# A new order for the chunks of the linear-attention heads in a two-layer hybrid decoder step

## The reference

```
S_t = e^{g_t} S_{t-1} + beta_t k_t (v_t - e^{g_t} S_{t-1}^T k_t)^T,   o_t = S_t^T q_t

# by chunks: q, k, v are the chunk's rows, gc the running sum of g in the chunk
decay = exp(gc_i - gc_j) for i >= j, else 0
L     = strictly lower part of (beta * k) k^T * decay
A     = L + I
u     = A^{-1} (v * beta)
w     = A^{-1} (k * beta * exp(gc))
qk    = (q k^T) * decay
# carried from chunk to chunk
v_new = u - w S
o     = (q * exp(gc)) S + qk v_new
S     = S * exp(gc_last) + (k * exp(gc_last - gc))^T v_new
```

## Time and profile before

| | us |
|---|---|
| median of 3 runs | 3143.12 |
| lowest and highest | 3142.41, 3145.15 |
| profiled execution, its own time | 3144.2 |
| span of the profiled execution | 3142.5 |
| TensorE busy in the span | 2954.7 (94%) |
| VectorE busy | 1398.7 (45%) |
| ScalarE busy | 610.6 (19%) |

### The profile page before, as it was taken

One profiled execution on the slowest core, in us unless ns is written; L12 is line 12 of the kernel. 1 busy time (PEld: TensorE's weight loads), 2 busy tenths in 40 slices (PEclk: granted clock), 3 DMA queues, 4 the chain that ended last, 5 costly groups with the idle time before them and its releaser, 6 DMA issues.

```text
span 3142.5 us, 46028 instructions
## 1 busy us (share of the span) xinstructions
PE 2954.7 (94%) x16570; PEld 2409.3 (77%) x16570; DVE 1398.7 (45%) x2838; ACT 610.6 (19%) x1253; POOL 172.5 (5%) x207
## 2 busy tenths in 40 slices
PE   7999999998888899999989999999988889999997
PEld 5888888887765578888778888888886656788885
DVE  5444545116554244445354453450365542544544
ACT  1101002123364311110010000121234542111000
POOL 3000000000032000000000000000002320000000
PEclk9999999989999999999999999999898989999998
DMA  8432222220068733222233312222103685222122
GB/s 166 127 84 76 61 88 67 67 68 17 31 209 241 209 94 81 80 80 61 71 101 86 87 51 74 77 81 67 58 0 123 224 232 164 67 81 80 56 82 66
DMA packets 366169, 301.16 MB, mean 96 GB/s; under 512 B 14738, under 2 KB 338540, under 8 KB 365842
## 3 DMA queue, kind: packets, MB, share of 16 engines
q1 hardware_dynamic: 341756, 217.98, 24.8%
q0 software_dynamic: 24256, 81.11, 8.8%
HBM read 287.21 MB, written 14.45 MB: 96 GB/s over the span
## 4 chain that ended last, share of the span: by engine, by line
PE 87%; DVE 4%; ACT 3%; DMA 2%; issue 2%; DVEq 1%; SPq 0%; POOL 0%; ACTq 0%; POOLq 0%
PE banks L702 25%; PE banks L795 17%; PE banks L852 13%; PE banks L727 5%; PE banks L738 5%; PE banks L666 4%; PE banks L1288 3%; PE banks L967 2%; PE banks L971 2%; PE banks L959 1%; DMA arena<-in_cache_v,layer_cache_rows 1%; DMA keys_values_by_token<-in_w_gate 1%; PE banks L1119 1%; ACT arena L1366 1%; PE banks L1183 1%
## 5 line engine op out<-in xcount | busy, mean ns | idle before, releaser
L852 PE MATMUL banks<-normed_or_mixed,weight_slots 128*128 128x272 f32 x1792 | 413.5, 393 | 2.3 <-DVE normed_or_mixed L1769 2.3
L852 PEld LDWEIGHTS banks<-normed_or_mixed,weight_slots 128*128 128x128 f32 x1792 | 340.4, 190 | 73.1 <-DVE normed_or_mixed L1769 3.2
L702 PE MATMUL banks<-normed_or_mixed,arena 128*128 128x272 f32 x1408 | 337.8, 393 | 5.4 <-DVE arena L1821 5.4
L702 PE MATMUL banks<-arena 128*128 128x272 f32 x1408 | 337.0, 392 | 0.0
L702 PEld LDWEIGHTS banks<-normed_or_mixed,arena 128*128 128x128 f32 x1408 | 267.0, 190 | 63.2 <-DVE arena L1821 3.8
L702 PEld LDWEIGHTS banks<-arena 128*128 128x128 f32 x1408 | 267.6, 190 | 55.0
L1366 ACT ACTIVATE hidden_or_projected<-banks 128x1024 f32<-128x1024 f32 (+4 forms) x160 | 137.1, 864 | 224.8 <-PE banks L666 147.5
L795 PE MATMUL banks<-hidden_or_projected,keys_values_by_token 128*128 128x272 f32 x704 | 177.0, 392 | 0.0
L795 PE MATMUL banks<-arena,keys_values_by_token 128*128 128x272 f32 x704 | 169.6, 393 | 1.1 <-DVE arena L1878 1.1
L795 PE MATMUL banks<-hidden_or_projected,weight_slots 128*128 128x272 f32 x704 | 169.2, 392 | 0.0
L795 PEld LDWEIGHTS banks<-arena,keys_values_by_token 128*128 128x128 f32 x704 | 133.5, 190 | 30.0 <-DVE arena L1878 2.8
(11 more groups left out here) (372 smaller groups left out, 4263.8 us busy)
## 6 DMA issues: line engine op xcount, KB each, us to landing
weight_slots<-in_w_down SPq DMA_DIRECT2D x128, 256.0 KB
weight_slots<-in_w_in SPq DMA_DIRECT2D x28, 1024.0 KB
keys_values_by_token<-in_w_gate SPq DMA_DIRECT2D x48, 512.0 KB, 5.0
keys_values_by_token<-in_w_up SPq DMA_DIRECT2D x48, 512.0 KB, 5.2
weight_slots<-in_w_gate SPq DMA_DIRECT2D x40, 512.0 KB, 5.0
weight_slots<-in_w_up SPq DMA_DIRECT2D x40, 512.0 KB, 5.1
hidden_or_projected<-in_cache_win_k SPq DMA_DIRECT2D x112, 128.0 KB, 4.5
weight_slots<-in_w_down SPq DMA_DIRECT2D x64, 192.0 KB
```

The lines of the kernel that those rows point to most:

```text
L702: mm = pe.matmul(ps[:, bank, 0:HALF], weights[:, k, :], acts[:, k, :], start=first and k == 0, stop=k == 3, skip_group_check=True)
L852: mm = pe.matmul(half(bank + 2 * u, h), wslot[:, slot, at:at + 128], hT[:, k, h * HALF:(h + 1) * HALF], start=k == 0, stop=k == KD - 1)
```

## The change

The work of a chunk stays the same, instruction for instruction, except for one more small copy; its order and its banks change.

- VectorE: the copy into T comes right behind `lower`, ahead of the state's update (`inverse_start`); QKT follows the state's update (`queries_by_keys`, with a new semaphore `qkt`); the scaling of the queries comes between level 1 and level 2 (`scaled_queries`).
- ScalarE: `eG` is computed with the other decays of the next chunk, while the chunk before is still being worked on. The twelve scaled copies are cut in four, three behind the copies of M in each of levels 1 to 4. Ahead of the first three, a small copy `etot` keeps the last column of `eG` for the state's update. The loop over levels is written out.
- TensorE: the first level is written out. M goes to banks 4 and 5, the correction of U to 7 and 6. In level 1 the first pair's corrections wait for `state_done` (the state's increment is in bank 7) and the second pair's for `qkt` (bank 6).
- The semaphore `in_strip` goes; its one load counts on `in_rows`, and the one wait for it moves a few lines down to the wait for `in_rows`.

```diff
@@ setup @@
         sign = small[:, 152:153]
+        etot = small[:, 153:157]
...
-            st(strips[:, :, :], bass.AP(tensor=skewed.tensor, offset=127, ap=[[SKEW, 128], [128 * (SKEW + 1), 8], [1, SEQ]]), "in_strip")
+            st(strips[:, :, :], bass.AP(tensor=skewed.tensor, offset=127, ap=[[SKEW, 128], [128 * (SKEW + 1), 8], [1, SEQ]]), "in_rows")
@@ TensorE, chunk @@
-                def level(k, last=False):
+                def level(k, first=False, last=False):
                     for a in range(2):
                         pe.wait_ge(s["t_up"], it * 12 + k * 2 + a - 1)
                         for i in range(2):
-                            mm = pe.matmul(ps[:, 4 if a else 7, 128 * i:128 * i + 128], m["LK"][:, 2 * a + i, :],
+                            mm = pe.matmul(ps[:, 4 + a, 128 * i:128 * i + 128], m["LK"][:, 2 * a + i, :],
                                            m["T"][:, 2 * a + i, :], start=True, stop=True)
                         mm.then_inc(s["m_mm"], 1)
                     for a in range(2):
+                        if first and a == 0:
+                            pe.wait_ge(s["state_done"], l * 5 + c + 1)
+                        if first and a == 1:
+                            pe.wait_ge(s["qkt"], it + 1)
                         pe.wait_ge(s["m_sb"], it * 12 + k * 2 + a - 1)
...
-                            mm = pe.matmul(ps[:, 5 + a, 128 * i:128 * i + 128], m["M"][:, 2 * a + i, :],
+                            mm = pe.matmul(ps[:, 7 - a, 128 * i:128 * i + 128], m["M"][:, 2 * a + i, :],
                                            m["U"][:, 2 * a + i, :], start=True, stop=True)
...
-                with pe.Fori(1, 6) as k:
+                level(1, first=True)
+                with pe.Fori(2, 6) as k:
                     level(k)
@@ ScalarE, decays (of the next chunk) @@
                 act.activation(kde[:, :], kde[:, :], ACT.Exp).then_inc(s["exp_done"], 1)
-
-            def scaled(l, c):
-                it = l * 4 + c
-                act.wait_ge(s["state_done"], l * 5 + c + 1)
-                alone(act)
                 act.activation(m["eG"][:, :, :], ps[:, 2, :].rearrange("p (h n) -> p h n", h=4), ACT.Exp)\
                     .then_inc(s["exp_done"], 1)
-                act.wait_ge(s["bege"], it + 1)
-                act.wait_ge(s["tokm"], it + 1)
-                for h in range(NH):
-                    hs = slice(128 * h, 128 * h + 128)
-                    copy(m["KB"][:, h, :], ps[:, 0, hs], bege[:, h:h + 1])
-                    copy(m["KD"][:, h, :], ps[:, 0, hs], kde[:, h:h + 1])
-                    last = copy(m["VB"][:, h, :], ps[:, 1, hs], m["bB"][:, h, 0:1])
-                last.then_inc(s["kv_done"], 1)
+
+            def scaled(l, c, h):
+                it = l * 4 + c
+                if h == 0:
+                    act.wait_ge(s["state_done"], l * 5 + c + 1)
+                    act.wait_ge(s["bege"], it + 1)
+                    act.wait_ge(s["tokm"], it + 1)
+                    alone(act)
+                    copy(etot, m["eG"][:, :, 127])
+                hs = slice(128 * h, 128 * h + 128)
+                copy(m["KB"][:, h, :], ps[:, 0, hs], bege[:, h:h + 1])
+                copy(m["KD"][:, h, :], ps[:, 0, hs], kde[:, h:h + 1])
+                last = copy(m["VB"][:, h, :], ps[:, 1, hs], m["bB"][:, h, 0:1])
+                if h == NH - 1:
+                    last.then_inc(s["kv_done"], 1)
@@ ScalarE, chunk @@
-                with act.Fori(1, 7) as k:
+                for k in range(1, 7):
                     for a in range(2):
                         act.wait_ge(s["m_mm"], it * 12 + k * 2 + a - 1)
-                        copy(m["M"][:, 2 * a:2 * a + 2, :], two(4 if a else 7)).then_inc(s["m_sb"], 1)
+                        copy(m["M"][:, 2 * a:2 * a + 2, :], two(4 + a)).then_inc(s["m_sb"], 1)
+                    if k <= NH:
+                        scaled(l, c, k - 1)
...
-                if more:
-                    scaled(l, c + 1)
@@ VectorE @@
-            def begin(l, c):
+            def inverse_start(l, c):
                 it = l * 4 + c
-                dve.wait_ge(s["kkqk"], it * 2 + 2)
-                dve.tensor_tensor(m["QKT"][:, :, :], m["DT"][:, :, :], four(6), ALU.mult)
                 dve.wait_ge(s["t_mm"], it + 1)
                 dve.wait_ge(s["rows_out"], l * 160 + 160)
                 cp(m["T"][:, :, :], four(5)).then_inc(s["t_up"], 2)
+
+            def queries_by_keys(l, c):
+                it = l * 4 + c
+                dve.wait_ge(s["kkqk"], it * 2 + 2)
+                dve.tensor_tensor(m["QKT"][:, :, :], m["DT"][:, :, :], four(6), ALU.mult).then_inc(s["qkt"], 1)
+
+            def scaled_queries(l, c):
+                it = l * 4 + c
                 dve.wait_ge(s["exp_done"], it * 2 + 2)
                 dve.tensor_tensor(m["qc"][:, :, :], m["qc"][:, :, :], m["eG"][:, :, :], ALU.mult)
...
-                        dve.tensor_tensor(m["U"][:, hs], m["U"][:, hs], two(5 + a), ALU.subtract).then_inc(s["u_up"], 1)
+                        dve.tensor_tensor(m["U"][:, hs], m["U"][:, hs], two(7 - a), ALU.subtract).then_inc(s["u_up"], 1)
...
-                with dve.Fori(1, 6) as k:
+                level(1)
+                scaled_queries(l, c)
+                with dve.Fori(2, 6) as k:
                     level(k)
...
+                if more:
+                    inverse_start(l, c + 1)
                 dve.wait_ge(s["s_mm"], it + 1)
                 for h in range(NH):
-                    last = stt(m["S"][:, h, :], m["S"][:, h, :], m["eG"][:, h, 127:128], ps[:, 7, 128 * h:128 * h + 128],
+                    last = stt(m["S"][:, h, :], m["S"][:, h, :], etot[:, h:h + 1], ps[:, 7, 128 * h:128 * h + 128],
                                ALU.mult, ALU.add)
                 last.then_inc(s["state_done"], 1)
                 if more:
-                    begin(l, c + 1)
+                    queries_by_keys(l, c + 1)
@@ VectorE, attention @@
                     if n == 3:
-                        dve.wait_ge(s["in_strip"], 16)
...
-                        dve.wait_ge(s["in_rows"], 16 * 7 * T_S)
+                        dve.wait_ge(s["in_rows"], 16 * (7 * T_S + 1))
```

More of the change, by code:

```diff
@@ L128 @@
     "comb", "conv_acc", "conv_done", "conv_in", "conv_in_mm", "conv_rows", "conv_rows_mm", "conv_tail", "cv_in0",
[L129 removed]
+    "cv_in1", "cv_in2", "cv_in3", "decay_mm", "qkt", "delta_out", "down_free", "dn_prod", "dn_out", "dn_mix", "dn_one", "t_down", "dt_arg", "dt_exp",
     "exp_done", "gb", "gdone", "gmm", "gsq", "gsqrt", "h_done",
     "mix_done", "mix_out", "one_done", "prod", "t_mix", "g_silu", "wg_in0", "wg_in1", "wu_in0", "wu_in1", "hid_done", "in_bias", "in_start", "in_lam",
[L132 removed]
+    "in_pages", "in_rows", "in_vec", "k_free", "kkqk", "ks_mm", "kt_sb", "kt_in", "kv_done",
     "lam_exp", "lam_sums", "layer_vecs", "m_mm", "m_sb", "mu_mm", "new_mm", "new_sb", "nw_sb", "o_mm", "o_out",
@@ L1691, in _ @@
                 decays(l, 0)
-                scaled(l, 0)
                 with act.Fori(0, 3) as c:
@@ L2382, in _ @@
                 lower(l, 0)
-                begin(l, 0)
+                inverse_start(l, 0)
+                queries_by_keys(l, 0)
                 with dve.Fori(0, 3) as c:
```

2 lines of the change are left out of this document (removed).

## The result

| | before | changed | ratio, 95% interval |
|---|---|---|---|
| first series, median (runs) | 3147.30 us (13) | 3129.31 us (13) | 0.9947, 0.9935 to 0.9958 |
| second series | 3149.60 us | 3131.92 us | 0.9938, 0.9918 to 0.9958 |
| third series | 3149.39 us | 3133.62 us | 0.9950, 0.9935 to 0.9964 |
| fourth series | 3144.84 us | 3127.12 us | 0.9943, 0.9928 to 0.9958 |

The change makes the kernel faster by 16 to 18 us; 26.7 us were forecast, and 3129.3 lies above the range that ended at 3126. The profiled execution of the changed kernel took 3126.44 us, with a span of 3124.8. One execution of 8379.58 us in the first series was disturbed; it is left out of the ratio, though the median of 13 still counts it.

The account below looks back on a forecast made before the run. TensorE, busy 94% of the span, bounds the kernel; time is lost in idle gaps and half clock between chunks. 26.1 plus 0.6 off the profiled 3144.2 gives 3117.5, for the median 3116.4 us; range 3111 to 3126.

Parts of the forecast that it names:

- The passages: Six chunk-to-chunk stretches of the linear heads, turned U to level 2: 27.1 us instead of 53.20, a gain of 26.1.
- The margins: Level 1 to 2: VectorE has T ready 0.23 us before TensorE wants it; at worst 3.3 us lost over six passages.
- the rival with M waiting on ScalarE: Levels 1 to 4: scaled copies between the copies of M make levels late; slower, up to 3173 us; 4 in 100.
- the one in the attention heads: Cache loads set the attention heads' pace, so the gain is given back there; about 3143 us; 4 in 100.
- Together 26.7: Whole gain forecast in us: 26.1 from the six passages plus twice 0.3 from chunk 0 of each layer.
- chunk 0 and what surrounds it: Chunk 0 of each layer: only the earlier copy into T counts, level 1 begins 0.3 us sooner, 0.6 in both.
- the rival with the clock falling all the same: Level 1 of the passages: corrections stay at half clock, 9.0 us comes back, 3125.4 us; 12 in 100.

Follow-up runs that it names:

- e2: Changed kernel with VectorE's old order (state's update, QKT, then the copy into T), scaled copies still spread; 3138.10 us, ratio 0.9963 to the kernel before.
- e6: Changed kernel with two of six levels left out per chunk, scaled copies in sixes behind levels 1 and 2; 3074.14 us, 0.9767 to the kernel before.
- e13: Kernel before with level 1 written out on TensorE and VectorE and all six levels on ScalarE, orders unchanged; 3158.35 us, ratio 1.0040.
- e17: Changed kernel with ScalarE's levels 2 and 3, and 5 and 6, in loops again; 3123.93 us, ratio 0.9922 to the kernel before.
- e18: Changed kernel with those ScalarE loops and matmuls added ahead of chunk 0's turned keys and turned inverse; 3123.67 us, 0.9921 to the kernel before.
- e3: Changed kernel with all scaled copies in one block ahead of the copies of M and a ScalarE drain; 3168.71 us, 1.0060 to the kernel before.
- e15: Kernel before with only ScalarE's six levels written out; 3152.49 us, ratio 1.0002.
- e16: Kernel before with only level 1 written out on TensorE and VectorE, ScalarE's loop kept; 3153.66 us, ratio 1.0019.
- e11: Kernel before with sixteen unread matmuls added at its two gaps, five ahead of level 1, eleven behind its first products; ratio 1.0020.
- e12: Changed kernel with unread matmuls added in chunk 0, nine ahead of the turned keys, eleven ahead of the turned U; 3123.21 us, 0.9916 to the kernel before.
- e4: Changed kernel with eleven unread matmuls added in the 2.70 us idle ahead of chunk 0's turned U; ratio 0.9940 to the kernel before.
- e7: Changed kernel with twenty unread matmuls added in chunk 0 and seven in the sample group's chunk; 3122.84 us, 0.9915 to the kernel before.
- e8: Changed kernel with two matmuls added ahead of W and four behind the sample group's decays, in chunk 3; one execution, 3128.08 us.

## Why the prediction was too low

3129.3 is 12.9 us above the forecast 3116.4.

*The passages* were right as a mechanism and nearly in size: 25.0 of the 26.1 us forecast. The copy into T begins 0.10 us after L667 ends (forecast 0.13), L960 comes 1.44 after L667 began (1.47), the copies of M no longer wait for the scaled ones, the clock is at 1.00, and the two corrections take 1.89 (1.88). Only L972 is off: it comes 1.42 after L960 instead of 1.17. The state's update, which it waits for now, ends at 751.90, 0.45 ahead of it. In e2, where that update ends before the copy into T begins, the distance is 1.37, so the new wait is hardly the reason; in the first level M is copied 0.75 after L960 begins against 0.65 in the earlier trace rows, and the rest of it was not taken apart. The price is 0.2 us a passage.

*The margins* held. VectorE, forecast 0.23 us ahead, does not hold up level 2: L960 there shows no idle time. Levels 2 to 5, with three scaled copies behind M in three of them, take 3.05 each, as without them, so the rival with M waiting on ScalarE has no trace. Nor has the one in the attention heads: 209.4, 212.8 and 210.3 us in the first layer before, 209.5, 211.5, 207.2 and 213.3 after, and e6 agrees.

*Two terms of the sum failed, and a third is open. The first is the clock outside the passages, put at nothing for all that comes after level 2.* "Together 26.7" took everything after level 2 as it was. Measured in the first pair of traces: 25.0 from the passages, 0.9 from chunk 0 and what surrounds it (0.6 forecast), 2.9 lost at the end of chunk 3: 23.0. The clock was weighed at the passages and at chunk 0, nowhere else. Of the rival with the clock falling all the same, the place was wrong and the sign right. The rule weighed there (the Trainium skill, "TensorE: Matmul & The Clock Gate", section "A second HAM failure mode: psum-queue depth-cycling": short idles between groups of matmuls make the clock swing) would have had the passages at half clock; their row shows 1.00 behind 0.84 us of idle time. At the end of chunk 3 the granted clock falls with no idle time in the window ahead of it; the nearest, 0.51 us ahead of W, stands in the kernel before as well, and there the clock stays up. Short idles do not explain that.

*The second is the base.* The forecast stood on the median of the three runs shown, 3143.1; the 13 of the first series have 3147.3. That alone is 4.2 us, and the range had no term for it. On the base of 3147.3 the range would have ended at 3130 and held the 3129.3, but by luck: the forecast gain would still have been 8.7 us too large.

*The remainder.* 4.2 of base and 3.7 of the linear heads leave 5.0 of the 12.9. They are the difference between the traces' 23.0 and the timed gain of 18.0 in that series. The other three series, with 15.8 to 17.7 us against 22.4, lack 5 to 7 as well. A part is that the traced executions of the changed kernel were quick ones: its four took 3127.1 us on average and all 29 on record 3130.2, while the three traced of the kernel before took 3148.0 and 89 on record 3149.2. That makes 2 us of difference between traces and timed runs. The prediction took nothing for the levels written out. The code's form can cost as much as is lacking and more (e13, 12.6 us by the ratio), and e17 suggests that here it does; e18 speaks against so simple an account. The rest stays open.

## What to carry to other kernels

Where one engine idles between stages, list what its supplier does first and what it could do later: here most of the gain came from twelve copies that nobody needed yet, and advancing the other instruction without moving them made the kernel slower (e3). After such an edit, read the granted clock in every stretch that follows and not only where the idle time was. And a sum made against one execution needs a term for what the untouched stages do from one execution to the next: here 10 us, against a timed gain of 16 to 18. One trace also says little about a difference in timed runs when the traced execution is a quick or a slow one: put its own time beside the median first.

## What the runs showed of the hardware

- Half clock without idle time in front: after 2.4 us of 32-row matmuls the granted clock was 0.53 for 3.6 us in the changed kernel and 1.00 in the one before, with the same instructions. It fell in all eight such stretches of the changed kernel's four traces (10.98 to 11.36 us) and in none of the twelve of the kernel before and of e13, e15 and e16 (9.73). Added matmuls far ahead of the stretch turned it either way: it fell in both of e11 and in neither of e12, and fell in one layer of e4 (12.49) and not in the other (9.73). What decides it was not found.
- A single gap of 1.93 us left the clock at full in five of six passages (e2); two gaps, 1.93 and 1.81, had it fall in all six of the kernel before, and one of 3.90, behind one of 0.84, in all six of e3.
- Matmuls whose result nobody reads held the clock in idle time, at about 0.24 us each in float32 (2.62 for eleven). They paid in chunk 0's gap of 2.70 us (e7, e12) and not in one of 1.81 (e11); around the sample group's decays they did not hold it (e8).
- Writing out loops changed the median by 0.4% (e13, interval 0.26% to 0.55%); the profiled execution was the quickest of its six and does not show where.
- Executions of one program, timed side by side, differ by up to 20 us (3140.4 to 3159.1), and the mean granted clock goes with the time: 2.4 to 2.5 us for 0.001.
